# Leaving out the products at the norms whose result nobody reads

## What is computed

```python
def rmsnorm(x, gain):
    xf = x.astype(jnp.float32)
    y = xf * lax.rsqrt(jnp.mean(xf * xf, axis=-1, keepdims=True) + EPS)
    return (y * gain.astype(jnp.float32)).astype(x.dtype)

for i in range(DEPTH):
    h = rmsnorm(x, norm1_g[i]) * (1.0 + sc1) + sh1
    x = x + g1 * attention(h)
    h = rmsnorm(x, norm2_g[i]) * (1.0 + sc2) + sh2
    x = x + g2 * swiglu(h, w_gate[i], w_up[i], w_down[i])
...
    u = rmsnorm_2(h, norm_mix_w[l])
    h = h + hybrid_mixer(u, ...)
    v = rmsnorm_2(h, norm_ffn_w[l])
    h = h + conv_gated_mlp(v, ...)
return rmsnorm_2(h, final_norm_w)
```

## Time and profile before

| | us |
|---|---|
| median of 3 runs | 2427.55 |
| lowest and highest | 2424.36 to 2430.35 |
| the profiled execution, its own time | 2431.22 |
| its span in the profile | 2429.4 |
| PE busy | 2314.1 (95%) |
| DVE busy | 1227.2 (51%) |
| ACT busy | 874.0 (36%) |

### The profile page before, as it was taken

The page is one execution under the profiler, slowest core; times in us unless marked ns, Lnnn a source line. Parts: engine busy times, 40 slices in busy tenths (PEclk is TensorE's granted clock), DMA queues, the critical chain, the costliest instruction groups (busy, mean ns, idle before and its releaser), DMA issues.

```text
span 2429.4 us, 27096 instructions
## 1 busy us (share of the span) xinstructions
PE 2314.1 (95%) x10968; PEld 1830.4 (75%) x10968; DVE 1227.2 (51%) x1761; ACT 874.0 (36%) x1452; POOL 201.6 (8%) x146
## 2 busy tenths in 40 slices
PE   3888999999999999999999999999999999999998
PEld 2555778888876767888887887767768887888887
DVE  6787556453346564433334546456654335553453
ACT  1554322222244443331232224553653323332332
POOL 6200100000100001000001000121120001000001
PEclk9998899999999999999999999999999999999999
DMA  6333255552221211323222322212123222232222
GB/s 250 117 116 128 68 182 203 178 214 91 99 73 53 70 53 52 105 96 102 98 96 78 98 101 88 104 62 70 61 87 108 96 100 79 96 104 96 87 95 78
DMA packets 70973, 250.91 MB, mean 103 GB/s; under 512 B 7872, under 2 KB 8000, under 8 KB 70848
## 3 DMA queue, kind: packets, MB, share of 16 engines
q1 hardware_dynamic: 70848, 249.17, 30.0%
HBM read 244.95 MB, written 4.19 MB: 103 GB/s over the span
## 4 chain that ended last, share of the span: by engine, by line
PE 82%; DVE 8%; ACT 6%; issue 2%; POOL 1%; DMA 0%; SPq 0%; DVEq 0%; POOLq 0%; ACTq 0%
PE pb L717 24%; PE pb L721 24%; PE pb L719 24%; DVE slab L1317 2%; ACT whi L1026 1%; PE pb L762 1%; DVE wlo L1294 1%; PE pb L912 1%; PE pb L887 1%; DVE slab L1345 1%; ACT hhi L1054 1%; PE pb L739 1%; DVE hlo L1351 1%; PE pb L740 1%; PE pb L741 1%
## 5 line engine op out<-in xcount | busy, mean ns | idle before, releaser
L717 PE MATMUL pb<-hhi,whi 128*128 128x512 f32 x1976 | 799.8, 405 | 4.9 <-ACT hhi L1054 3.0
L1294 DVE TENSOR_TENSOR wlo<-raw,whi 128x1024 fp32r<-128x1024 f32 x361 | 449.5, 1250 | 678.2 <-ACT whi L1026 678.0
L719 PE MATMUL pb<-hhi,wlo 128*128 128x512 f32 x1976 | 774.7, 392 | 2.1 <-DVE wlo L1294 2.1
L721 PE MATMUL pb<-hlo,whi 128*128 128x512 f32 x1976 | 774.8, 392 | 0.7 <-DVE hlo L1351 0.7
L1026 ACT ACTIVATE whi<-raw 128x1024 fp32r<-128x1024 f32 x361 | 378.7, 1055 | 710.1 <-PE pb L721 674.8
L717 PEld LDWEIGHTS pb<-hhi,whi 128*128 128x128 f32 x1976 | 372.9, 189 | 114.8 <-issue 41.2
L721 PEld LDWEIGHTS pb<-hlo,whi 128*128 128x128 f32 x1976 | 372.7, 189 | 84.4 <-DVE hlo L1351 3.5
L719 PEld LDWEIGHTS pb<-hhi,wlo 128*128 128x128 f32 x1976 | 373.7, 189 | 78.8 <-issue 3.8
L717 PE MATMUL pb<-ahi,whi 128*128 128x512 f32 x848 | 336.8, 397 | 3.6 <-ACT ahi L1186 2.2
L721 PE MATMUL pb<-alo,whi 128*128 128x512 f32 x848 | 331.6, 391 | 0.0
L719 PE MATMUL pb<-ahi,wlo 128*128 128x512 f32 x848 | 331.3, 391 | 0.0
(11 more groups left out here) (198 smaller groups left out, 1809.1 us busy)
## 6 DMA issues: line engine op xcount, KB each, us to landing
raw<-stream SPq DMA_DIRECT2D x361, 512.0 KB, 3.2
slab<-ada_w SPq DMA_DIRECT2D x80, 512.0 KB, 4.5
early<-ada_w SPq DMA_DIRECT2D x16, 512.0 KB, 13.4
X<-xT SPq DMA_DIRECT2D x8, 256.0 KB, 6.8
ya<-slab SPq DMA_DIRECT2D x8, 256.0 KB, 2.5
slab<-ya SPq DMA_DIRECT2D x8, 256.0 KB, 4.8
outT<-X SPq DMA_DIRECT2D x8, 256.0 KB, 2.1
cst<-consts SPq DMA_DIRECT2D x1, 646.5 KB, 3.8
```

Of the source, the lines that this page charges most:

```text
L717: e.matmul(out, wh, hi, start=s.k == 0, stop=False)
L719: e.matmul(out, wl, hi, start=False, stop=False)
L721: i = e.matmul(out, wh, lo, start=False, stop=s.last)
L1294: e.tensor_tensor(wlo[:, u % NW, :], raw[:, u % NRAW, :], whi[:, u % NW, :].bitcast(F), ALU.subtract).then_inc(*v_cut.up(u))
```

## The change

The ticks `warm` are left out of `norm` and of the end of `score()`: three for each of five norms and two at the last, 17 in all. Nothing else is touched; the function that makes them stays in the program but is not called. Of reading, splitting and products the order stays.

```diff
@@ -195,11 +195,8 @@
     def norm(n):
-        tick("warm", 1)
         rstd(n)
-        tick("warm", 1)
         tick("spread", n)
-        tick("warm", 1)
         for k in range(KD):
             tick("norm", n, k)
```

## The result

| | before | after |
|---|---|---|
| median of 8 runs, us | 2427.70 | 2433.82 |
| lowest and highest | 2424.36 to 2431.88 | 2431.26 to 2434.98 |
| profiled execution, its own time | 2431.22 | 2434.98 |
| granted clock, mean of the span | 0.983 | 0.979 |

The kernel without the 17 products takes 1.0024 times as long, 95% interval 1.0013 to 1.0034: 6.1 us more by the medians. That is slower, though by less than the 0.3% that the prediction called distinguishable, and half of what the forecast of 2440 meant against this median. Only one of the eight executions of before was longer than the shortest of after.

A forecast was written before the change was run, and what follows sets the result against it. TensorE, busy 95% of the span, was taken to bound the kernel. Five norms at 3.0 us, 15.1 in all, less 5.9 already paid, gave +9.2 us on the profiled 2431.2, so 2440; range 2432 to 2446.

The forecast's parts named there:

- the base of the sum: Whole kernel: the rise was added to the profiled execution's 2431.2 us, which stands 3.7 us above the median of 2427.55.
- the net at the norms: At the five norms: 15.1 us lost without the products, less 5.9 already paid before, +9.2 us.
- The 17 products are hidden: At all norms: the products lie in PE's waits for other engines, so removing them gains 0, at most 1 us.
- The banks and the other engines: PSUM bank waits move to other takes, worth 0; nothing moves on DVE, ACT, POOL or SP.
- The clock falls at every norm without them: At norms 1 to 5: PE, idle without the products, drops from 2.4 to 1.2 GHz before the broadcast.
- The broadcast, 0.93 us: At each norm, broadcast to DVE's first tile takes 2.09 us at half clock, 1.16 at full: 0.93 lost.
- The one-column sums, 0.2 us a norm: Sums before the broadcast take 1.85 us at half clock against 1.05: 0 to 0.8 lost, 0.2 taken.
- The products behind, 1.9 us a norm: Behind each norm, half clock lasts 4.1 us into the block's products at 0.47 us lost per microsecond: 1.9 us.
- what before paid: Half-clock losses already in the kernel before: 2.0, 3.2 and 0.75 us at norms 1 to 3, together 5.9.
- Same: Outcome for the whole kernel: a difference under 0.3%, about 7.3 us, not distinguishable from none; chance 0.17.
- the one with the clock that doesn't care: Rival: the products may decide nothing about PE's clock at the norms; time 2427 to 2431 us, chance 0.14.
- the slow one: Rival: at every norm the clock falls before the sums and returns late, +14.2 us, 2445; chance 0.10.

The follow-up runs named there:

- two middle: The kernel before with two unread products instead of one between sums and broadcast, 23 in all: 2425.36 us, ratio 0.9990; again 2421.69 us, ratio 0.9988.

## Why the prediction was right and wrong

The direction, the mechanism at the norms and the range (2432 to 2446) held; the size didn't. The forecast of 2440 is 12.3 us above the median of before, and 6.1 were measured. Two steps failed, the base of the sum and the way of a loss to the end of block 1. Of the 6.6 us between 2440.4 and 2433.8 the base is 3.5 and the net at the norms 1.9; 1.2 stay without a place. That 2433.8 still lies in the range is no merit of the sum: the range was wide, and its low end allowed for the base.

**The 17 products are hidden: right.** Worth 0 each, and the gaps of norm(1) and (2), at half clock in both traces, are the same to 0.01 us. The queue was never on the path, not even by the 0.05 and 0.15 us allowed for.

**The banks and the other engines: right.** No new wait in any block.

**The clock falls at every norm without them: right**, 5 of 5, and 10 of 10 in the three traces that have such norms.

**The broadcast, 0.93 us: right**, 0.92, 0.92, 0.65, 0.93 and 0.91 against two middle; norm(3) fell in the middle of it.

**The one-column sums, 0.2 us a norm: wrong.** They cost nothing: L773 to DVE's scaling is 1.09 us at every norm, as before. L773 took 1.05 us at all five norms of the trace after, its length at full clock, so the clock hadn't fallen by then. Of 15.1 the term is 1.0 too much.

**The products behind, 1.9 us a norm: wrong in block 1, in part in block 3, and a little too high in the others.** The half clock held for 5.5, 4.5, 3.7, 6.1 and 4.2 us, 4.8 in the mean and longer than the 4.1 I took, yet it cost 0.0, 1.7, 0.7, 2.6 and 1.8 us, 6.9 in all for the 9.5 of the sum. Block 1 is the place where the step failed, and block 3 in part: I carried PE's loss to the end of the block without asking what PE waits for next. The prediction had the stop itself in view, the window from 315.38, and read it only for the clock behind it. The 4.38 us before it were PE's slack for everything that went before. The same holds in the account of what before paid: 1.1 of its 2.0 us at norm(1) never reached the end.

Another reading of that stop was a little off, without changing a price. The prediction has PE restart there at half clock. PE started again at 312.59 at full clock, and the clock fell 0.7 us later:

```profile
312.59:313.27 0.68, 0.68 (x7) 0.68 (x7) 0.68 (x1) 0.00 (x0) 0.00 (x0) 1.00 1.01 398
313.27:315.38 2.11, 2.11 (x12) 2.11 (x12) 0.31 (x1) 0.00 (x0) 0.00 (x0) 0.50 0.97 348
```

In sum a norm without the products cost 2.3 us in the mean of five, 11.3 in all, where the prediction had 15.1; before paid 4.0 in its profiled execution, where it had 5.9. The net at the norms is 7.3, for 9.2.

**The base: wrong, and the largest part of the error.** I made the sum on the profiled execution, 3.5 us above the median of all eight. The prediction named the alternative, 2436.7 from the median, and passed over it by supposing that the other executions have more norms like (4) and (5), so that the rise against them would be larger. They don't have many more: outside that profile 8 of 15 norms held, where it had 2 of 5, and the second profile of before paid 2.8 us at its norms, little less than 4.0. The execution was slow by its clock: it had 82 us at half clock where 69.5 is the mean, and at 0.26 us for each that is 3.3 of the 3.5 us. Only 20 of the 82 lay at norms 1 to 5. Another 38 lay ahead of norm(1), where the twelve traces have between 20 and 44 us and the start of norm(1) follows them (correlation 0.77). Which part made this execution longer than the typical one isn't known. From the median, 2427.7, and the measured net of 7.3 one comes to 2435.0. The 1.2 us between that and 2433.8 are within the uncertainty of the medians.

**The chances.** "Same", a difference under 0.3%, had 0.17 and is what came, 0.24%; the eight runs of each kernel still tell it from none, which the prediction had ruled out under 0.3%. Of the rivals, the one with the clock that doesn't care is out (5 of 5 norms, two middle), and so is the slow one, since the clock never fell before L773 and the products behind the norms lost 6.9 us, not its 11.5. The Trainium skill's sentence on the page "TensorE: Matmul & The Clock Gate", section "What's actually happening", that activity releases the low clock, agrees with the third product's effect: 0 to 2.2 us of half clock behind four of five norms with it, where 3.7 to 6.1 stood without any. The remark of the Trainium skill in the same section that the number of slow products varies from run to run agrees too: the same kernel had 43 to 92 us of half clock.

What isn't settled is why a norm with all three holds in one execution and not in the next. No experiment here set it.

## What to carry to other kernels

Work that nobody reads can be free and useful at once: ask for each such instruction which wait it lies in, and what it does to the clock, and price a loss of clock only up to the next place where that engine waits for another. When a time scatters with the granted clock, make the sum on the median and its typical clock, not on the one execution that was profiled.

## What the runs showed that I had not expected

The product behind the broadcast is worth more than the two before it: with it alone the clock, though it falls, is back when the block begins, or 0.1 us later, at three norms of five, and 2429.5 us are measured against 2433.8. The scatter of this kernel goes with its clock: 0.26 us for each microsecond at half clock, with correlation 0.96 over 53 executions. And leaving out all the filler made the kernel slower but more even: its eight executions lie between 2431.3 and 2435.0, those of before between 2420.6 and 2433.5 over some ninety. That fits a clock that falls at every norm instead of at some, but the even clock of the norms wasn't tested as the cause.
